# Expert gathers that bring two picks of 64 tokens, multiplied in the two column halves of TensorE

## The reference, cut to what matters

```python
def one(xb):
    q = (xb @ wq).reshape(blk, PEER_HEADS, 2, PEER_DK_HALF)
    s = jnp.einsum('thpc,hpnc->thpn', q, subkeys).astype(jnp.float32)
    sv, si = lax.top_k(s, PEER_TOPK)
    cand = (sv[:, :, 0, :, None] + sv[:, :, 1, None, :]).reshape(blk, PEER_HEADS, PEER_TOPK * PEER_TOPK)
    cidx = (si[:, :, 0, :, None] * N_KEYS + si[:, :, 1, None, :]).reshape(blk, PEER_HEADS, PEER_TOPK * PEER_TOPK)
    fv, fi = lax.top_k(cand, PEER_TOPK)
    eidx = jnp.take_along_axis(cidx, fi, axis=-1)
    gate = jax.nn.softmax(fv, axis=-1)
    act = jax.nn.gelu(jnp.einsum('thkd,td->thk', pu[eidx], xb), approximate=False) * gate
    return jnp.einsum('thk,thkd->td', act, pv[eidx])
```

## Time and profile before

| | |
|---|---|
| median of three runs | 2175.59 us |
| the profiled execution's own time | 2169.85 us |
| its span | 2168.0 us |
| busy: TensorE, VectorE, GpSimd, ScalarE | 1836.0, 1407.4, 889.1, 503.5 us |
| moved by DMA | 733.36 MB, mean 338 GB/s |
| indirect gathers' share of the DMA engines | 63.1% of the span |
| the chain that ended last | PE 39%, DMA 26%, DVE 12%, issue 8%, POOL 6% |

### The profile page before, as it was taken

The page is one execution under the profiler, slowest core; times in us unless marked ns, Lnnn a source line. Parts: engine busy times, 40 slices in busy tenths (PEclk is TensorE's granted clock), DMA queues, the critical chain, the costliest instruction groups (busy, mean ns, idle before and its releaser), DMA issues.

```text
span 2168.0 us, 25093 instructions
## 1 busy us (share of the span) xinstructions
PE 1836.0 (85%) x8048; PEld 1023.1 (47%) x8048; DVE 1407.4 (65%) x3247; ACT 503.5 (23%) x1339; POOL 889.1 (41%) x646
## 2 busy tenths in 40 slices
PE   6999978878878987888898888889898996776776
PEld 4546447546665653454465345446533552221222
DVE  4246766555359875657987565798756568674764
ACT  2112212111122321222232122223212222221221
POOL 0276770312016542434554334466424344443442
PEclk9999988988989999999899999999999999998999
DMA  8377747966668999999899999989999999999996
GB/s 285 128 265 243 222 127 235 326 221 219 224 233 308 382 391 415 413 406 414 318 390 385 415 399 416 403 331 383 384 398 355 416 396 369 410 416 394 408 416 274
DMA packets 169986, 733.36 MB, mean 338 GB/s; under 512 B 17757, under 2 KB 18606, under 8 KB 103154
## 3 DMA queue, kind: packets, MB, share of 16 engines
q0 software_dynamic: 75024, 545.82, 63.1%
q1 hardware_dynamic: 94834, 185.96, 24.9%
HBM read 722.69 MB, written 9.12 MB: 338 GB/s over the span
## 4 chain that ended last, share of the span: by engine, by line
PE 39%; DMA 26%; DVE 12%; issue 8%; POOL 6%; SPq 5%; ACT 2%; another core or an unknown queue 0%; DVEq 0%; ACTq 0%; POOLq 0%
PE bank L469 38%; DMA RING<-in_peer_uv,R 17%; DMA R<-in_peer_uv,R 7%; DVE RING L2028 4%; POOL MV L2193 3%; SPq L2290 3%; SPq L2349 2%; DVE R L2028 2%; POOL R L2193 1%; ACT R L1295 1%; DMA R<-h2s_d 1%; PE bank L476 1%; POOL RING L2270 1%; DMA RING<-in_w_mod 1%; DMA RING<-samp_d 1%
## 5 line engine op out<-in xcount | busy, mean ns | idle before, releaser
L469 PE MATMUL bank<-RING,R 128*128 128x512 f32 (+1 forms) x1560 | 756.9, 619 | 153.8 <-ACT R L1295 141.1
L2270 POOL DMA_INDIRECT RING<-in_peer_uv,R x390 | 455.0, 1167 | 730.4 <-PE bank L469 624.7
L469 PE MATMUL bank<-R 128*128 128x128 f32 (+5 forms) x2216 | 477.0, 366 | 83.5 <-ACT R L1295 67.5
L469 PEld LDWEIGHTS bank<-RING,R 128*128 128x128 f32 (+1 forms) x1560 | 279.9, 193 | 484.3 <-issue 470.1
L469 PEld LDWEIGHTS bank<-R 128*128 128x128 f32 (+3 forms) x2216 | 307.7, 194 | 277.2 <-issue 273.4
L2028 DVE SCALAR_TENSOR_TENSOR RING<-RING,R 128x1024 f32<-128x1024 f32 x192 | 251.6, 1312 | 139.5 <-DMA RING<-in_peer_uv,R 137.0
L2028 DVE SCALAR_TENSOR_TENSOR RING<-RING,MV 128x1024 f32<-128x1024 f32 x192 | 239.8, 1249 | 149.5 <-DMA RING<-in_peer_uv,R 146.3
L1285 ACT ACTIVATE R<-R 128x2 f32<-128x2 f32 x256 | 52.1, 203 | 1079.7 <-DVE RING L2028 878.1
L2270 POOL DMA_INDIRECT R<-in_peer_uv,R x130 | 155.5, 1196 | 212.3 <-PE bank L469 207.8
L1295 ACT ACTIVATE R<-ident,R 128x128 f32<-128x128 f32 x512 | 173.5, 386 | 0.3
L469 PEld LDWEIGHTS bank<-HT,R 128*128 128x128 f32 x1024 | 134.0, 196 | 47.6 <-issue 46.5
(11 more groups left out here) (310 smaller groups left out, 1696.0 us busy)
## 6 DMA issues: line engine op xcount, KB each, us to landing
R<-in_peer_wq SPq DMA_DIRECT2D x16, 2048.0 KB
RING<-in_w_mod SPq DMA_DIRECT2D x12, 2048.0 KB, 8.2
MV<-in_cache_k SPq DMA_DIRECT2D x88, 256.0 KB, 3.7
R<-in_cache_v SPq DMA_DIRECT2D x84, 256.0 KB, 3.6
R<-in_w_out SPq DMA_DIRECT2D x6, 2048.0 KB
MV<-in_cache_v SPq DMA_DIRECT2D x44, 256.0 KB, 3.8
RING<-in_w_in SPq DMA_DIRECT2D x5, 2048.0 KB, 9.4
R<-in_cache_k SPq DMA_DIRECT2D x40, 256.0 KB, 3.6
```

What stands on the lines that cost most here:

```text
L469: i = nc.tensor.matmul(out, lhsT, rhs, start=start, stop=stop, **k)
L2270: nc.gpsimd.indirect_dma_start(UV[g % UN], None, a["peer_uv"][0], bass.IndirectOffsetOnAxis(ap=idx, axis=0)).then_inc(S(f"uv_in{g % UN}"), 16)
```

## The change

The four tiles keep their 128 tokens, but a gather now brings two picks (k = 2m and 2m + 1) of 64 tokens, where it brought one pick of 128. Steps 2m and 2m + 1 of a unit together bring the same 256 rows as before: the even step those of tokens 0 to 63, the odd step those of tokens 64 to 127; partitions 0 to 63 hold the one pick and partitions 64 to 127 the other. For this

- `picks` writes the indices, and `gate_scale` the gates, in four blocks of 64 x 8 (two halves of tokens by two parities of picks), where each was one operation of 128 x 16;
- the dot products need a tile's rows twice over: `halves` on ScalarE copies tokens 64 to 127 into both halves of H2HIGH (it takes the place of G2S) and then tokens 0 to 63 over the upper half of H2; even steps multiply with H2, odd ones with H2HIGH, and the first dot of a tile waits for the copies;
- the stationary operand is 128 x 64: a folded identity (1 in row r, column r mod 64) scaled by the weights, so that one product adds the two picks of each of 64 tokens;
- `value_pair` runs at the even steps, for both: the even step's products write partitions 0 to 63 of the bank, the odd one's partitions 64 to 127, interleaved. The steps of the sample tokens stay as they were;
- G2S, the gate rows of the sample tokens, moves to G1S, and is loaded later.

```diff
+PAIRED = 4
...
+        G2S = G1S
...
-        G2, G2S, FW = MV[:, 0, :], MV[:, 1, :], MV[:, 2, :]
+        G2, H2HIGH, FW = MV[:, 0, :], MV[:, 1, :], MV[:, 2, :]
+        FOLD = hide_q[:, 0:64]
...
+        DGH = part(R1, 11960, 256, n=4, c=64)
+        GATS = part(R1, 12216, 64, t=4, n=16)
...
+            def value_pair(g, n, s_):
+                t, h = divmod(n, PH)
+                k = n * STEPS + s_
+                lo, hi = banks[(t % 2) * 2], banks[(t % 2) * 2 + 1]
+                first, last = h == 0 and s_ == 0, h == PH - 1 and s_ == STEPS - 2
+                if first and t >= 2:
+                    pe.wait_ge(S("sums_taken"), t - 1)
+                for b in range(2):
+                    pe.wait_ge(S(f"uv_in{(g + b) % UN}"), 16 * ((g + b) // UN + 1))
+                pe.wait_ge(S("diagonal"), k + 2)
+                for bank, at in ((lo, 1024), (hi, 1536)):
+                    for b in range(2):
+                        mm(bank[64 * b:64 * b + 64, :], DGH[:, (k + b) % 4, :], UV[(g + b) % UN][:, at:at + 512], first, last,
+                           S("v_used") if bank is hi else None)
...
-                elif n is not None:
+                elif n is not None and n >= PAIRED * PH:
                     value_step(g, n, s_)
+                elif n is not None and g % 2 == 0:
+                    value_pair(g, n, s_)
...
+            def halves(t):
+
+                low, high = h2_rows(t)[0:64], h2_rows(t)[64:P]
+                act.wait_ge(S("h_ready"), nth_h2(t) + 1)
+                job_done(act, ("h2T", t, 1))
+                if t:
+                    act.wait_ge(S("dots"), at_step[t * PH - 1, STEPS - 1] + 1)
+                A(H2HIGH[64:P], high, ACT.Copy).then_inc(S("half_rows"), 1)
+                A(H2HIGH[0:64], high, ACT.Copy).then_inc(S("half_rows"), 1)
+                act.wait_ge(S("half_rows"), 3 * t + 2)
+                A(high, low, ACT.Copy).then_inc(S("half_rows"), 1)
...
-                A(DG[:, k % 4, :], ident[:, :], ACT.Copy, scale=AG[:, n % 4, s_:s_ + 1]).then_inc(S("diagonal"), 1)
+                dst, ones_ = (DGH, FOLD) if n < PAIRED * PH else (DG, ident[:, :])
+                A(dst[:, k % 4, :], ones_, ACT.Copy, scale=AG[:, n % 4, s_:s_ + 1]).then_inc(S("diagonal"), 1)
...
+                if c == 0:
+                    halves(0)
...
+                if n is not None and n % PH == s_ == 0 and 0 < n < PAIRED * PH:
+                    halves(n // PH)
...
+            step(V.tensor_tensor(FOLD, ident[:, 0:64], ident[:, 64:P], ALU.add))
+            blocks = [(a_, b) for a_ in range(2) for b in range(2)]
...
+                for a_, b in blocks:
+                    dst, src_ = slice(64 * a_, 64 * a_ + 64), slice(64 * b, 64 * b + 64)
+                    step(V.scalar_tensor_tensor(eix[dst, b:16:2], R01[src_, 0, a_:16:2], float(NKEY), R01[src_, 1, a_:16:2], ALU.mult, ALU.add))
...
-                    dve.wait_ge(S("h_ready"), nth_h2(n // PH) + 1)
+                    if n < PAIRED * PH:
+                        dve.wait_ge(S("half_rows"), 3 * (n // PH) + 3)
...
-                    V.scalar_tensor_tensor(u, u, 1.0, H2[n // PH % 2], ALU.mult, ALU.mult, accum_out=DOT[:, n % 4, s_:s_ + 1]).then_inc(S("dots"), 1)
+                    V.scalar_tensor_tensor(u, u, 1.0, H2HIGH if s_ % 2 and n < PAIRED * PH else H2[n // PH % 2], ALU.mult, ALU.mult, accum_out=DOT[:, n % 4, s_:s_ + 1]).then_inc(S("dots"), 1)
...
+                    for a_, b in blocks:
+                        dst, src_ = slice(64 * a_, 64 * a_ + 64), slice(64 * b, 64 * b + 64)
+                        step(V.tensor_scalar(GATS[dst, x, b:16:2], GAT[src_, x, a_:16:2], SUMG[src_, x:x + 1], None, ALU.mult))
+                    settle()
...
-            load(G2S[0:NB], mod_d[1:9, 5 * D_MODEL:6 * D_MODEL], "g2_in")
...
                     store(h2s_d, HS2[0:NB, :], "h2s_out")
+                    load(G2S[0:NB], mod_d[1:9, 5 * D_MODEL:6 * D_MODEL], "g2_in")
```

More of the change, by code:

```diff
@@ L1935, in _, with picks @@
             step(V.tensor_copy(IOTA16, IOTAI))
+            step(V.tensor_tensor(FOLD, ident[:, 0:64], ident[:, 64:P], ALU.add))
             job_done(dve, ("oT", 3, 1))
             settle()
-            def picks(n, src, fv, eix):
+            blocks = [(a_, b) for a_ in range(2) for b in range(2)]
+            def picks(n, src, fv, eix, paired=False):
                 rows = slice(0, n)
@@ L1989, in picks @@
                 settle()
-                step(V.scalar_tensor_tensor(eix, R01[rows, 0, :], float(NKEY), R01[rows, 1, :], ALU.mult, ALU.add))
+                if not paired:
+                    step(V.scalar_tensor_tensor(eix, R01[rows, 0, :], float(NKEY), R01[rows, 1, :], ALU.mult, ALU.add))
+                    return
+                for a_, b in blocks:
+                    dst, src_ = slice(64 * a_, 64 * a_ + 64), slice(64 * b, 64 * b + 64)
+                    step(V.scalar_tensor_tensor(eix[dst, b:16:2], R01[src_, 0, a_:16:2], float(NKEY), R01[src_, 1, a_:16:2], ALU.mult, ALU.add))
             def prompt_picks(n):
@@ L1996, in prompt_picks @@
                 x = n % 4
-                yield from picks(P, QT[:, 2 * h:2 * h + 2, 0:P], FVS[:, x, :], EIX[:, x, :])
+                yield from picks(P, QT[:, 2 * h:2 * h + 2, 0:P], FVS[:, x, :], EIX[:, x, :], t < PAIRED)
                 step(V.tensor_scalar(NMX[:, x:x + 1], FVS[:, x, 0:1], -1.0, None, ALU.mult))
@@ L2091, in sample_sums @@
             def sample_sums():
+                dve.wait_ge(S("g2_in"), 48)
                 dve.wait_ge(S("v_used"), at_step[SAMPLES, NB - 1] + 1)
```

10 lines of the change are left out of this document (7 added, 3 removed).

## The result

The changed kernel takes 2191.47 us (median of 4 runs, 2183.76 to 2198.62), the kernel before 2171.60 us on the same chip (4 runs, 2163.89 to 2178.64). The ratio is 1.0101, 95% interval 1.0066 to 1.0137: 20 us slower, where I forecast 28 us faster. Its profiled execution took 2183.76 us (span 2182.0).

What follows compares the result with a forecast made beforehand. DMA was taken to set the pace in the clean part, TensorE where over half the gain lay; -17.1 - 6.4 - 5.2 + 2 + 2 - 3.2 = -27.9 us gave 2148 us, range 2135 to 2162, eight in ten 2126 to 2183.

Steps and rivals of the forecast that it cites:

- the rival on the clock: Last tile: less busy TensorE may run at 1.2 GHz, no loss unless slot work slows too, then 2235 us; 5%.
- the first comes some 0.4 us earlier or later: Ring slots: a pair releases both steps' buffers within 0.5 us, the first some 0.4 us earlier or later than before.
- I take 417 GB/s as the floor of the whole stage.: Gather stage: the rate at 1850 to 1950 us, DMA share 1.01, as the limit from which stretches' losses were computed.
- The delta stretches, -17.1: Stretches solving the next tile's delta rule: TensorE's relief wins back 60% of their 28.5 us loss, -17.1 us.
- a change of width: TensorE between pairs and slots: 0.14 us each, 327 changes; rival with 1.15 us each gives 2211 us, 6%.
- My own sign of being wrong: Wrong if delta stretches stay at 380 GB/s with TensorE idle; forecast there was over 400 GB/s.
- in the 30% that VectorE idles: VectorE's additions, 1.1 us a unit, 35 us over 32 units, hide there where DMA sets the pace.
- delta, output projection and queries together: Three kinds of stretches where TensorE's relief wins 17.1, 6.4 and 5.2 us; bounds together 0 and 49.6.
- The end: Last sixteen value passes in the chain: 7.12 us become 3.9 as pairs, -3.2 us.
- Tile starts: ScalarE copies +4 (bounds 0 and 10.5), VectorE's additions +4, TensorE's relief -6: together +2 us.
- The gain is hidden: Rival: DMA itself is slower in the delta stretches, or VectorE follows at once; 2166 us, 20%.
- VectorE becomes the pace: Rival: VectorE's additions 1.8 us a unit, 3.5 at each tile's start, none of the delta loss won; 2188 us, 9%.

Runs made afterwards that it cites:

- e3: Changed kernel with two full-width products that nobody reads added behind every pair of the last tile; 2181.85 us, ratio 1.0051.
- e7: Changed kernel with ten gather buffers instead of eight in the last tile; 2154.24 us, ratio 0.9955 to the kernel before.
- e8: Kernel before with ten gather buffers instead of eight in the last tile; 2158.58 us, ratio 0.9959.
- e5: Changed kernel with full-width products (half the stationary columns zero), both of the even step ahead of both of the odd; 2190.23 us, ratio 1.0119.
- e9: Kernel before with only VectorE's added instructions and the added wait; 2187.38 us, ratio 1.0037.
- e1: Changed kernel with the last tile as before, without pairs; 2172.66 us, ratio 1.0021.
- e10: Changed kernel, ten buffers in the last tile, single VectorE instructions instead of four, permutation left out (outputs not the reference's); 2154.93 us, ratio 0.9900.
- e14: Kernel before, no pairs, with ten buffers in the last tile and gates scaled on ScalarE; 2161.10 us, ratio 0.9915.
- e12: Changed kernel, ten buffers in last tile, single VectorE instructions, permutation and ScalarE's row copies left out (outputs not the reference's); 2153.14 us, ratio 0.9895.
- e15: Changed kernel, ten buffers in the last tile, permutation on ScalarE, pair's products in order of steps; 2148.39 us, ratio 0.9862.
- e16: Changed kernel, ten buffers in the last tile, permutation on ScalarE, first gather started earlier; 2149.40 us, ratio 0.9844.
- e6: Kernel before with full-width value products of two steps together, low half of both, then high half of both; 2212.93 us, ratio 1.0225.
- e4: Changed kernel with both column-half products of the even step ahead of both of the odd; 2193.02 us, ratio 1.0127.

## Why the prediction was wrong

**The step that failed** is the one in the rival on the clock. I saw that TensorE might run at 1.2 GHz in the last tile, and wrote "a pair then takes 3.44 us of 5.02, as much as now, no loss". The length was right (3.46 and 3.56 us). "No loss" compared busy time with the time of two gathers. What counts is when the first buffer goes back, and there 3.5 us for a pair isn't the same as 3.67 us for two steps one after the other: 4.3 us after the start, where it was 2.2. The same mistake is in "the first comes some 0.4 us earlier or later", which holds at the full clock only. The last tile became 26 us longer: 19.5 go when the clock is brought back (e3), and all of it goes with two more buffers (e7 against e8). The 6.5 that e3 leaves are near the 8 of e5; VectorE's additions make up 4 of them by e9, the rest is not taken apart.

The Trainium skill ("TensorE: Matmul & The Clock Gate", HAM oscillation — how this bites in real kernels) describes bursts of products that are short against the wait for DMA, whose clock falls again in each wait. The trace agrees in part: the pairs at 1901.97 and 1908.43 us, with 2.9 us of waiting ahead of them, ran at 0.53 and 0.54, but the clock did not fall in every wait (the pair at 1913.32, behind 1.43 us, had 1.00). The Trainium skill counts the slower products as the loss; here the loss came through the buffers they held.

**"I take 417 GB/s as the floor of the whole stage."** Wrong: e7 and e8 move 421, and the last tile of the kernel before is 10 us shorter with ten buffers. A share of 1.01 didn't prove that DMA set the pace: it stood beside 405 GB/s (1700 to 1800), beside 417, and beside 421 in e7. That DMA set the pace in the last tile was nearly right all the same: 417 is 1% under the 421.

**The delta stretches, -17.1.** TensorE did what I worked out. Timeline of the changed kernel, beside the earlier trace rows:

```profile
1076.05 1.94 PE L474 MATMUL bank<-RING,R 128*64 128x512 f32 x8 [1.28 <-ACT R L1330]
1077.91 2.05 PE L474 MATMUL bank<-R 128*128 128x128 f32 x16
1079.89 1.94 PE L474 MATMUL bank<-RING,R 128*64 128x512 f32 x8
1081.76 2.05 PE L474 MATMUL bank<-R 128*128 128x128 f32 x16
1086.29 3.51 PE L474 MATMUL bank<-RING,R 128*64 128x512 f32 x8 [2.48 <-ACT R L1330]
```

From 1076.05 to 1079.89 a pair and its slots take 3.84 us; I had 3.78, two changes of width included. So the price of a change of width, 0.14 us, was about right (0.17 by these rows), and that rival is out. But the time did not follow. From the sums of tile 0 to those of tile 2 the four executions with this code (changed, e1, e3, e7) took 767.7, 775.6, 784.8 and 771.4 us, the two with that of before (before, e8) 772.8 and 771.2. My own sign of being wrong, delta stretches at 380 GB/s with TensorE idle, came true in most of them. TensorE's relief only uncovered the next thing. The chain of waits of the changed kernel in this stretch, where the earlier trace rows had one piece of TensorE of 38 us:

```profile
1078.22 8.67 DMA RING<-in_peer_uv,R
1086.91 1.76 DVE RING L2078 x2
...
1090.98 1.16 DVE RING L2078 x2
1092.19 0.07 issue
1092.27 0.58 ACT R L1330 x2
1092.85 0.14 issue
1092.99 1.96 PE bank L474 x8
1094.94 0.22 issue
1095.16 8.00 DMA R<-in_peer_uv,R
```

This is a loop through the ring: a landing of 8.67 us, then 6.1 us of VectorE and ScalarE until the pair starts (1086.91 to 1092.99), 2 us of products, and the next gather; 16.9 us from gather to gather (1078.22 to 1095.16). Between the pair that let the first gather go (1076.05) and the one at its end (1092.99) stand three pairs, six steps, so the loop gives a step every 2.8 us, which is 372 GB/s (an estimate from these rows; the window of the stretch has 393). VectorE is the fullest engine in it, with 14.6 of 16.9 us. In such a loop an added microsecond on VectorE can count, although VectorE has idle time. That is the second failed step: I hid its additions "in the 30% that VectorE idles". The groups of the changed kernel by line and form, beside the earlier trace rows:

```profile
L2091 DVE TENSOR_SCALAR R<-R 64x8 f32<-64x8 f32 x128 | 41.2, 322 | 4.2
L2037 DVE SCALAR_TENSOR_TENSOR R<-R 64x8 uint32<-64x8 f32 x128 | 23.9, 187 | 4.1
```

They add 45.8 us, 1.43 us a unit, where I took 1.1; of this 8 us show in the kernel before (e9) and 12 with the pairs (e10 against e7). What the pairs win once both faults are gone is 12 to 13 us (e14). I had 28.7 for delta, output projection and queries together. In the changed kernel as it is, nothing of it arrived (e7 against e8); with VectorE relieved the direction is right and the size over twice too large. The output projection stayed at 385 GB/s; what holds it there I haven't taken apart.

**Smaller terms.** The end: -1.8 us (7.12 to 5.37), not -3.2, because the last sixteen passes still ran in good part at the low clock (3.9 us were forecast for them at the full one). Tile starts: VectorE waited 8.7 us in all for ScalarE's copies, near the 10.5 at most that I gave, but e12 shows no cost. TensorE's busy time fell by 275 us, not 350 to 450; the low clock accounts for it, since the value products' rows hold 648 us and 256 pairs of 1.94 us would be 497.

**The sum, as measured.** Pairs -12 to -13 (e14 against e15 and e16), VectorE's additions +8 to +12 (e9, e10), the late release at the low clock in the last tile +19.5 (e3): +15 to +20, beside the measured +20 (14 to 30). The terms come from different kernels and may not add exactly. e1 shows it: without the late release they would give -5 to 0, and it measured +4.6, from -2 to +11. So the first three tiles are explained to some 8 us and no better, and single executions of the same code differ there by 18 us. One suspect was not tested: the pair at 1086.29 us above took 3.51 us, so the low clock reaches the first three tiles too, and filler was tried only in the last.

**The rivals.** "The gain is hidden" is what happened in the first three tiles ("VectorE follows at once") and gave 2166; it had no loss in it. "VectorE becomes the pace" gave 2188, 3 us from the measurement, by luck: its loss was to come from VectorE's additions and the tile starts. The additions did cost, but the loss that made the change slower than before lies in the last tile. "The clock" looked at the right tile and called it free. None of the five had the mechanism that decided: a lateness that is no busy time of any engine.

## What to carry to other kernels

With a ring of buffers, ask of a change when each buffer is given back, and not only how busy the engines are. A buffer's whole round (flight of its gather, wait for its use, use, wait for the next gather) is what counts: the number of buffers divided by the round is the rate. Steps that are put together with their neighbours lengthened the round here (e6). Check it at both levels of TensorE's clock, since work taken off TensorE can lower the clock. Before an engine is relieved, try one or two more buffers where room comes free: here that alone took 36.6 us off the changed kernel's last tile and 10 off that of the kernel before. Take two or three profiles of the same code before a gain of 10 us in a stretch is believed.

## What the runs showed of the hardware

- Work put in made a stretch faster: two unread products behind each pair raised the granted clock from 0.69 to 0.98 and shortened the last tile by 19.5 us (e3).
- Two column halves run fully side by side also when both products of one step stand ahead of those of the other (e4): a pair took 1.94 us in either order, at the full clock, and the last tile stayed within 6 us of the changed kernel's.
- A DMA share of 0.98 to 1.01 stood beside anything from 378 GB/s (changed kernel, 1850 to 1950) to 421 (e7). As a sign that DMA is the limit it is no use here.
- With two more buffers a gather took longer, while the rate rose little: 10.4 us in the chain of the changed kernel's last tile, 12.6 and 13.1 in that of e7, at 378 and 421 GB/s.
